# A normalised copy of the last feed-forward's input, and one unused 512-column product ahead of five stretches of 256-column products

## The reference

```python
def rms_norm_2(x, gain):
    xf = x.astype(jnp.float32)
    y = xf * lax.rsqrt(jnp.mean(xf * xf, axis=-1, keepdims=True) + EPS)
    return (y * gain.astype(jnp.float32)).astype(x.dtype)
...
        merged = (jax.nn.sigmoid(gate_a) * (o_a @ w_br_dsa[l])
                  + jax.nn.sigmoid(gate_b) * (o_b @ w_br_moba[l]))
        x = x + gt_m * (merged @ w_out[l])

        h = rms_norm_2(x, g_ffn_norm[l]) * (1.0 + sc_f) + sh_f
        g_ff, u_ff = jnp.split(h @ w_gate_up[l], 2, axis=-1)
        x = x + gt_f * ((jax.nn.silu(g_ff) * u_ff) @ w_down[l])
```

## Time and profile before

| what | value |
|---|---|
| median of 3 runs | 1469.18 us |
| lowest and highest run | 1468.82 us, 1470.86 us |
| span of the profiled execution | 1468.2 us |
| TensorE busy in it, products | 98%, 11585 |
| VectorE, ScalarE busy | 72%, 48% |

### The profile page before, as it was taken

How to read it: one execution, slowest core, us unless ns; L and a number is a source line. 1 busy time by engine, 2 the same in 40 slices (tenths; PEclk the granted TensorE clock), 3 DMA queues, 4 the chain that set the end, 5 groups by cost and what they waited for, 6 DMA issues and landing times. The chain is left out here.

```text
span 1468.2 us, 28465 instructions
## 1 busy us (share of the span) xinstructions
PE 1446.1 (98%) x11585; PEld 1406.6 (96%) x11585; DVE 1056.6 (72%) x1439; ACT 700.0 (48%) x910; POOL 29.0 (2%) x58
## 2 busy tenths in 40 slices
PE   8999999999999999999999999999999999999999
PEld 8999999999999999999999889999987899999999
DVE  6766779777667786677878768767887777876652
ACT  6544353454443454443554655443436766544431
POOL 0000100000001000001000000001000000000000
PEclk9999999999999999999999999999999999999999
DMA  9555835437447644458343226647633436365540
GB/s 324 220 187 186 268 149 201 172 106 267 172 172 249 239 173 172 171 196 288 128 173 124 78 70 246 227 173 268 234 115 135 145 139 231 131 228 185 184 173 30
DMA packets 42538, 269.09 MB, mean 183 GB/s; under 512 B 4768, under 2 KB 5920, under 8 KB 13520
## 3 DMA queue, kind: packets, MB, share of 16 engines
q1 hardware_dynamic: 33984, 240.31, 45.1%
q0 software_dynamic: 7312, 26.44, 5.5%
q10 hardware_dynamic: 1152, 1.05, 0.2%
HBM read 266.73 MB, written 1.05 MB: 182 GB/s over the span
## 5 line engine op out<-in xcount | busy, mean ns | idle before, releaser
L418 PE MATMUL ps<-x_hi,w_hi 128*128 128x272 f32 (+2 forms) x2296 | 661.8, 288 | 6.7 <-DVE x_lo L1447 1.9
L420 PE MATMUL ps<-x_hi,w_lo 128*128 128x272 f32 (+2 forms) x2296 | 651.8, 284 | 0.0
L419 PE MATMUL ps<-x_lo,w_hi 128*128 128x272 f32 (+2 forms) x2296 | 651.7, 284 | 0.0
L2024 ACT ACTIVATE w_hi<-raw_weights 128x2048 fp32r<-128x2048 f32 x219 | 416.9, 1912 | 291.6 <-PE ps L420 289.0
L1174 DVE TENSOR_TENSOR w_lo<-raw_weights,w_hi 128x2048 fp32r<-128x2048 f32 x193 | 439.7, 2288 | 143.8 <-ACT w_hi L2024 143.3
L418 PEld LDWEIGHTS ps<-x_hi,w_hi 128*128 128x128 f32 x2296 | 433.1, 189 | 10.8 <-DVE x_lo L1380 2.5
L419 PEld LDWEIGHTS ps<-x_lo,w_hi 128*128 128x128 f32 x2296 | 433.3, 189 | 0.7
L420 PEld LDWEIGHTS ps<-x_hi,w_lo 128*128 128x128 f32 x2296 | 433.1, 189 | 0.0
L418 PE MATMUL ps<-a_hi,w_hi 128*128 128x272 f32 x592 | 169.6, 286 | 0.0
L419 PE MATMUL ps<-a_lo,w_hi 128*128 128x272 f32 x592 | 169.6, 286 | 0.0
L420 PE MATMUL ps<-a_hi,w_lo 128*128 128x272 f32 x592 | 169.6, 286 | 0.0
(11 more groups left out here) (259 smaller groups left out, 1543.9 us busy)
## 6 DMA issues: line engine op xcount, KB each, us to landing
raw_weights<-w_units SPq DMA_DIRECT2D x226, 1024.0 KB, 4.9
mod_w<-mod_units POOLq DMA_DIRECT2D x48, 512.0 KB, 5.5
raw_weights<-w_units SPq DMA_DIRECT2D x4, 256.0 KB, 5.8
raw_weights<-w_units SPq DMA_DIRECT2D x2, 512.0 KB, 9.2
out<-h ACTq DMA_DIRECT2D x8, 128.0 KB, 1.9
h<-x_in SPq DMA_DIRECT2D x2, 272.0 KB, 4.1
h<-x_in SPq DMA_DIRECT2D x1, 544.0 KB, 8.0
tab<-tables POOLq DMA_DIRECT2D x1, 512.0 KB, 7.9
```

The source lines that it names most:

```text
L418: pe.matmul(dst, wh, hi, start=start, stop=False)
L419: pe.matmul(dst, wh, lo, start=False, stop=False)
L420: return pe.matmul(dst, wl, hi, start=False, stop=stop)
L2024: act.activation(w_hi[:, u % RING, :], raw[:, u % RING, :], ACT.Copy).then_inc(S["hi_ready"], 1)
```

## The change

Three things are changed.

The first is in `up 4`. While groups 0 to 2 run as before, VectorE makes `xn`, which is h times gain times `rstd`, for the 256 tokens of each of the 8 input tiles (`scale`); ScalarE adds the shift and rounds it to `xn_hi` (`shifted_high`); VectorE makes `xn_lo` (`shifted_low`). From group 3 on the products take `xn_hi` and `xn_lo` with 256 columns. The eviction of these groups needs no scaling: ScalarE takes the silu straight from PSUM (`direct`), and VectorE multiplies it with the up half from PSUM (`direct_eviction`). The loop has three turns instead of four, and groups 2 and 3 are written out.

The second is `long_product`: one product of 512 columns (two token tiles at once) into a bank that the next product starts afresh, so its result is never used. It stands at five places: ahead of group 2 of `up 3`, ahead of the eighth output tile of the first contraction tile in `down 3`, in `w_out` and in `down 4`, and ahead of group 4 of `up 4`.

The third is only in the text of `group`: the number of columns is a parameter.

```diff
+            def long_product(bank, u, x):
+
+                pe.matmul(ps[:, bank, :].rearrange("p (a n) -> p a n", a=2), w_hi[:, u % RING, 0:P], x[:, 0:2, 0:SEQ],
+                          start=True, stop=True)
...
             def gate_up(n, x_base, part=None):
                 st = stages["up", n]
                 first_groups(st, x_base, part)
+                if n == 3:
+                    pe.wait_ge(S["lo_ready"], st.u0 + 5)
+                    wait_bank(st, st.tile(2))
+                    long_product(st.bank(st.tile(2)), st.u0 + 4, x_hi)
...
+            def last_gate_up(x_base):
+                st = stages["up", 4]
+                first_groups(st, x_base)
+                group(st, 2, (x_hi, x_lo))
+                group(st, 3, (xn_hi, xn_lo), y_base=x_base + KT, cols=SEQ)
+                pe.wait_ge(S["lo_ready"], st.u0 + 9)
+                wait_bank(st, st.tile(4))
+                long_product(st.bank(st.tile(4)), st.u0 + 8, xn_hi)
+                with pe.Fori(1, 4) as i:
+                    group(st, 2, (xn_hi, xn_lo), i, cols=SEQ)
+                    group(st, 3, (xn_hi, xn_lo), i, cols=SEQ)
+                group(st, 10, (xn_hi, xn_lo), cols=SEQ)
...
-            k_outer(stages["down", 3], a_of[SEQ], A0["up", 3])
+            k_outer(stages["down", 3], a_of[SEQ], A0["up", 3], long_at=7)
...
-            k_outer(stages["w_out"], (z_hi, z_lo), A0["br"])
-            gate_up(4, X0["up", 4])
-            k_outer(stages["down", 4], a_of[SEQ], A0["up", 4])
+            k_outer(stages["w_out"], (z_hi, z_lo), A0["br"], long_at=7)
+            last_gate_up(X0["up", 4])
+            k_outer(stages["down", 4], a_of[SEQ], A0["up", 4], long_at=7)
...
+            def scale(k):
+
+                dve.scalar_tensor_tensor(xn[:, k, :], h[:, k, META:TOK], gain2[:, 8 + k:9 + k], rstd[:, 0:SEQ],
+                                         ALU.mult, ALU.mult).then_inc(S["full_ready"], 1)
+
+            def shifted_low(k):
+
+                dve.wait_ge(S["x_hi_ready"], c.up("x_hi_ready"))
+                dve.scalar_tensor_tensor(xn_lo[:, k, :], xn[:, k, :], mod[:, 24 + k:25 + k], xn_hi[:, k, :].bitcast(F32),
+                                         ALU.add, ALU.subtract).then_inc(S["x_ready"], 1)
...
+                dve.tensor_tensor(up, ps[:, b + 2:b + 4, 0:SEQ], pair_a[:, :, 0:SEQ], ALU.mult).then_inc(S["tile_evicted"], 2)
+                dve.wait_ge(S["a_hi_ready"], e + 1 + 2 * i)
+                k = bass.ds(2 * g + 4 * i, 2)
+                dve.tensor_tensor(a_lo_s[:, k, :], up, a_hi_s[:, k, :].bitcast(F32), ALU.subtract).then_inc(S["a_ready"], 2)
...
+                split_to(st.u0 + 5)
+                gated_eviction(4, 0, scaled=(0, 1), also=(2, 3))
+                split_to(st.u0 + 7)
+                gated_eviction(4, 1, scaled=(4, 5), also=(6, 7), low=(0, 1))
+                split_to(st.u0 + 9)
+                gated_eviction(4, 2, low=(2, 3, 4), then_low=(5, 6, 7))
+                split_to(st.u0 + 11)
+                direct_eviction(3)
...
+            def shifted_high(k):
+
+                act.wait_ge(S["full_ready"], c.up("full_ready"))
+                act.activation(xn_hi[:, k, :], xn[:, k, :], ACT.Identity, bias=mod[:, 24 + k:25 + k])\
+                   .then_inc(S["x_hi_ready"], 1)
...
+                split_to(st.u0 + 5)
+                gated(4, 0)
+                split_to(st.u0 + 6)
+                for k in range(4):
+                    shifted_high(k)
+                split_to(st.u0 + 7)
+                gated(4, 1, high=(4, 5))
+                split_to(st.u0 + 8)
+                for k in range(6, 8):
+                    shifted_high(k)
+                split_to(st.u0 + 9)
+                gated(4, 2)
```

More of the change, by code:

```diff
@@ L528, in slab, with k_outer @@
                                xs[0][:, k, 0:st.T], xs[1][:, k, 0:st.T], k == 0, False)
[L530 removed]
+            def k_outer(st, xs, a_base, done=(), done_units=0, busy=None, long_at=None):
                 for n in range(st.units):
@@ L1209, in gated_eviction @@
+            def gated_eviction(n, g, i=0, scaled=(), also=(), low=(), then_low=()):
                 st = stages["up", n]
@@ L1219, in gated_eviction @@
                 dve.tensor_tensor(up, ps[:, b + 2:b + 4, 0:C], bcast(rstd, C), ALU.mult).then_inc(S["tile_evicted"], 2)
+                for k in scaled:
+                    scale(k)
                 dve.wait_ge(S["tile_evicted"], st.evicted(t + 4) + 8 * i)
@@ L1229, in gated_eviction @@
                     up = pair_b[:, :, 0:T]
+                for k in also:
+                    scale(k)
+                for k in low:
+                    shifted_low(k)
                 dve.wait_ge(S["a_hi_ready"], e + 1 + 2 * i)
@@ L1233, in gated_eviction @@
                 dve.tensor_tensor(lo[:, k, 0:T], up, hi[:, k, 0:T].bitcast(F32), ALU.subtract).then_inc(S["a_ready"], 2)
+                for k in then_low:
+                    shifted_low(k)
             def gate_up(n, mod_work=iter(())):
@@ L2055, in gated @@
                     ins.then_inc(S["silu_done"], 1)
+                for k in high:
+                    shifted_high(k)
                 act.wait_ge(S["act_in_ready"], I0["up", n] + g + 1 + 2 * i)
```

73 lines of the change are left out of this document (62 added, 11 removed).

## The result

The changed kernel takes 1472.93 us in the median of 17 runs (1470.83 to 1477.83), the kernel before 1469.18 us in 17 runs (1465.08 to 1473.86). The ratio is 1.0027, with a 95% interval of 1.0017 to 1.0037: slower by 0.27%, with an interval that lies above 1 throughout. 1463.4 us was forecast. The profiled execution of the changed kernel spans 1471.1 us, 2.9 more than that of before.

A forecast was written before the change was run, and what follows sets the result against it. TensorE's list of products, busy 98% of the span, was taken as the bound. Savings of 5.04, 0.29, 2.38 and 0.77 us against costs of 1.3 and 1.4 gave -5.8 us: 1463.4 from 1469.2, range 1461.5 to 1469.8.

The forecast's parts named there:

- Its clock in the top tenth in every slice: Whole kernel: TensorE's clock was read as at its 2.4 GHz level throughout, with TensorE busy 98% of the span.
- Behind a 512-column product I take the tight rhythm.: Streams behind long products: 256-column products would start 0.1133 us apart, read from one case at 1176.18 us.
- up 3 and down 3 are tight already. There is nothing to gain: Both stages: already at 0.1133 us from 889 us on, so unchanged but for 0.26 us each.
- a rival with a chance of 0.08: up 3 and down 3: the long product starts the loose rhythm, 6.2 us lost, +6.4 in all, 1475.6 us; chance 0.08.
- up 4, 5.04 us.: up 4, groups 4 to 10: 672 products go from 0.1208 us to the tight rhythm, 5.04 us saved; 2.02 if loose.
- down 4, 2.38 us.: down 4: 528 loose products turn tight, 2.38 us saved, otherwise nothing.
- w_out, 0.77 us.: w_out: 171 products behind its long product turn tight, 0.77 us saved, otherwise nothing.
- The stall, 1.4 us.: up 4, group 3: TensorE waits 1.4 us for xn_lo ahead of the third contraction tile; bounds 0 and 4.8 us.
- The long products, 0.26 each.: Five places: each costs 0.26 us with the uneven starts behind it; 1.15 to 1.3 us together, 1.3 taken.
- The lighter eviction, nothing: up 4 from group 3: VectorE has 2 instructions instead of 5, worth nothing by itself because it was no bound.
- Nothing ahead of the change: Ahead of up 4's group 3: nothing changes apart from w_out, so TensorE starts that group at 1309.78 us.
- the rival that switches nothing: All stretches keep their rhythm: 2.02 + 0.29 us saved, 1.15 + 1.4 paid, +0.2 us, 1469.4 us; chance 0.17.

The follow-up runs named there:

- before_again: The kernel before, unchanged, executed once more; its profiled span was 1469.3 us, 1.1 more than the first trace.
- first two probes: Changed kernel with an unused long product ahead of every group; in the second, one product later in odd groups; one run each, no time given.
- after_no_early: Changed kernel without the long products of up 3 and down 3, xn_lo not moved; 1468.30 us, ratio to the kernel before 0.9980.
- after_192: Changed kernel with all five long products and xn_lo moved by 192 bytes; 1470.22 us, ratio to the kernel before 1.0004.
- xn_only: Changed kernel without any of the five long products, keeping the copy; 1467.67 us, ratio to the kernel before 0.9988.
- v2_rule_used: Changed kernel with xn_lo moved 192 bytes, xn_lo tiles 2 and 3 made early, long products only three in up 4's group 4; 1462.69 us, ratio 0.9964.

## Why the prediction was wrong

The reading of the trace of before was right in the main: two prices for one width, no wait, and the rhythm as the only large term. "Its clock in the top tenth in every slice" holds for the slices only, as `before_again` shows. Step by step:

- *"Behind a 512-column product I take the tight rhythm."* This is the step that failed. It rested on one case, where the stream ahead was of 512-column products. In the 18 cases of the first two probes in `up 3` the outcome went by what stood ahead: out of tight it was loose, 9 times of 9, and out of loose it was tight 8 times of 9. In the changed kernel only two of five long products left 0.1133 us behind them.
- *"up 3 and down 3 are tight already. There is nothing to gain"*, with 0.26 us each as the cost. The loss was named as a rival with a chance of 0.08. In the trace `up 3` lost 4.1 us; `down 3` was turned back to tight. Taking the two away gave back 4.6 us on the medians (`after_no_early`). That rival was right in its mechanism for `up 3` alone.
- *up 4, 5.04 us.* 672 products went to 0.1178, not 0.1133: by that 2.0 us saved, my lower bound. Here the failed step had a second cause, which I had not seen at all: xn_lo starts 192 bytes past a multiple of 256, and no execution with it there, or at 0 past, showed a tight group; at 128 past they followed the rule. With the stall and the rest, `up 4` saved 0.6 us.
- *down 4, 2.38 us.* Measured 2.1 with the long product's cost. The number is right, by luck: the stream arrived loose and at a good place (394 ns). In `after_192` and `after_no_early` the same long product found a tight stream (226 ns) and made it loose, and in `xn_only` `down 4` was tight without one.
- *w_out, 0.77 us.* Nothing: 398 ns, the place where a loose stream stays loose. 0.2 us lost.
- *The stall, 1.4 us.* Measured 1.1, at the predicted place, on the predicted instruction. VectorE started group 2's eviction 1.03 us behind the start of group 3 (1316.58 against 1315.55); I had worked out 1.2.
- *The long products, 0.26 each.* 0.226 to 0.236 to the next start, as bounded. *The lighter eviction, nothing*: nobody waited for it.
- *Nothing ahead of the change*: 0.5 us came ahead of `up 3`. `before_again` moved by 1.25 us there without any change, and the 17 traces reach `up 3` anywhere from 870.99 to 873.98 us, so this tells nothing of the change.

The range ended at 1469.8, "the rival that switches nothing"; that rival's own sum gives 1469.4. It left out the combination that came: one stretch turned the wrong way, one the right way, one barred, one left as it was.

## What to carry to other kernels

Where products of one shape run at two prices, count the starts and look for what turns one into the other before adding anything: an odd product acted as a toggle here and not as a reset, and one case in a trace does not tell these apart. A probe that repeats the suspected switch nine times in one stage settles in a single run what rounds of timing can't. Put a new buffer for a matmul's moving operand where the buffers start whose streams run at the better price, and try it: here a place 64 bytes off (192 in place of 128) went with 128.1 us for `up 4` in place of 123.8, in one trace of each. And where the runs of one kernel spread over 9 us, compare traces stretch by stretch, never the spans alone.

## What the runs showed of the hardware

- A stream of 256-column fp32r products with a new weight tile each, on one core at the full clock, has a tight rhythm (0.1133 us, even) and a loose one (0.1178 us, steps of 117, 118 and 118 ns, with a weight load of 192 instead of 188 ns once in three). It stays in either for hundreds of products.
- A 512-column product in a tight stream (225 or 226 ns to the next start) always left it loose, 9 times in the table above and each time that one stood in a tight stream in another trace. In a loose stream the outcome goes by its place in the period of three: 230 to 234 ns and tight, or 235 or 236 ns and still loose. This holds where the buffers allow a tight rhythm at all. Three long products, the second 49 products behind the first and the third 12 behind that, left a stream tight in `v2_rule_used`, as they had found it (226, 236, 230 ns). By the rule they would do so from any state; from a loose one it was not seen.
- The tight rhythm came in `up 4` only with the second moving operand 128 bytes past a multiple of 256. At 192 past the prices were 0.1178 or 0.1192, at 0 past 0.1178. No other place was tried, and whether it is the place or its likeness to the first operand's (modulo 512) stays open. By the layout in the code x_hi, x_lo, a_hi_s, a_lo_s, z_hi and z_lo are at 128 past too; that moving one of them would spoil its rhythm was not tried. Why the place matters, and what in TensorE holds the rhythm, stays open.
- Which rhythm `up 3` gets goes with one gap ahead of it, in all 17 traces: 164 to 167 ns and loose (3), 135 to 161 or 174 to 176 ns and tight (14).
- In `before_again` the granted clock was 0.51 from 16.7 to 20.1 us, behind a wait of 2.5 us: 18 products in that window for 30 in before, from 0.3 us ahead of the first trace to 1.2 us behind it.
- The Trainium skill ("TensorE: Matmul & The Clock Gate", section "Back-to-back issue gap") has a formula for the gap of an isolated product, which gives 0.1092 us for 256 columns at the full clock; in a stream of weight loads and products, it says, both set the spacing, and it has no figure for 256 columns there and no second rhythm. The streams here, each product with a new weight tile, ran at 0.1133 us at best.
